# Four weight blocks taken in two passes behind the norms, and row block 5 of the attention outputs split around the memory heads

## The reference, cut to what matters

```python
for layer in range(DEPTH_2):
    # layer 0: NSA attention (compressed, selected, window), layer 1: MoBA attention
    q, ..., qm = split_cols(x @ w_in, sizes)
    o_mem = memory_attention(qm, mem, w_mem_kv)             # four heads on 256 memory rows
    mix = jnp.concatenate([o_main, o_mem], axis=-1) @ w_out # 1024 rows of w_out: 768 main, 256 memory
    x = layer_norm(ALPHA * x + mix, ln1_g[layer], ln1_b[layer])
    a, b = jnp.split(x @ ffn_w_in[layer], 2, axis=-1)
    ffn = (jax.nn.gelu(conv(a)) * b) @ ffn_w_out[layer]
    x = layer_norm(ALPHA * x + ffn, ln2_g[layer], ln2_b[layer])
```

## Time and profile before

| what | value |
|---|---|
| median of 3 runs | 958.37 us (957.88 to 958.4) |
| the profiled execution | 958.25 us |
| its span, first to last instruction | 956.6 us |
| TensorE matmul busy | 928.9 us, 97% |
| VectorE busy | 659.4 us, 69% |
| ScalarE busy | 527.2 us, 55% |
| mean granted TensorE clock | 0.994 |

### The profile page before, as it was taken

How to read it: one execution, slowest core, us unless ns; L and a number is a source line. 1 busy time by engine, 2 the same in 40 slices (tenths; PEclk the granted TensorE clock), 3 DMA queues, 4 the chain that set the end, 5 groups by cost and what they waited for, 6 DMA issues and landing times.

```text
span 956.6 us, 19717 instructions
## 1 busy us (share of the span) xinstructions
PE 928.9 (97%) x7025; PEld 844.7 (88%) x7025; DVE 659.4 (69%) x1258; ACT 527.2 (55%) x967; POOL 65.6 (7%) x119
## 2 busy tenths in 40 slices
PE   7999999999999999989999999999999999999995
PEld 4899999999999988667899999998988699999995
DVE  6466666666767777985886666668577796666665
ACT  5455555555544567764755455556665565555553
POOL 1000000000000001550100000001000100000001
PEclk9999999999999999999999999999999999999998
DMA  7555555556566666323566555565654447555641
GB/s 240 183 180 190 175 178 183 171 195 225 186 195 191 243 214 200 116 62 110 176 200 240 189 187 194 189 196 174 189 183 158 157 159 237 188 197 185 195 157 44
DMA packets 48233, 172.98 MB, mean 181 GB/s; under 512 B 6032, under 2 KB 6480, under 8 KB 48061
## 3 DMA queue, kind: packets, MB, share of 16 engines
q1 hardware_dynamic: 44732, 159.78, 50.7%
q0 software_dynamic: 3456, 12.61, 4.3%
HBM read 171.29 MB, written 1.07 MB: 180 GB/s over the span
## 4 chain that ended last, share of the span: by engine, by line
PE 86%; DVE 7%; ACT 3%; issue 2%; DMA 1%; POOL 0%; SPq 0%; POOLq 0%; DVEq 0%; ACTq 0%
PE bank L1411 18%; PE bank L1412 18%; PE bank L1410 18%; PE ysum L1481 6%; PE ysum L1483 6%; PE ysum L1482 6%; DVE sb_wl L830 2%; PE bank L1530 1%; PE ysum L1537 1%; PE ysum L1544 1%; PE ysum L1458 1%; PE ysum L1462 1%; PE ysum L1459 1%; DMA sb_raw<-in_stream 1%; ACT sb_xh L463 1%
## 5 line engine op out<-in xcount | busy, mean ns | idle before, releaser
L1411 PE MATMUL bank<-sb_xl,sb_wh 128*128 128x256 f32 x1360 | 377.9, 278 | 0.0
L1412 PE MATMUL bank<-sb_xh,sb_wl 128*128 128x256 f32 x1360 | 375.8, 276 | 0.0
L1410 PE MATMUL bank<-sb_xh,sb_wh 128*128 128x256 f32 x1332 | 370.5, 278 | 1.4 <-DVE sb_wl L830 1.4
L830 DVE TENSOR_TENSOR sb_wl<-sb_raw,sb_wh 128x1024 fp32r<-128x1024 f32 x201 | 245.3, 1223 | 111.9 <-ACT sb_wh L436 110.6
L436 ACT ACTIVATE sb_wh<-sb_raw 128x1024 fp32r<-128x1024 f32 x201 | 211.2, 1055 | 102.4 <-PE ysum L1483 43.4
L1410 PEld LDWEIGHTS bank<-sb_xh,sb_wh 128*128 128x128 f32 x1332 | 250.2, 188 | 6.4 <-issue 4.1
L1412 PEld LDWEIGHTS bank<-sb_xh,sb_wl 128*128 128x128 f32 x1360 | 255.5, 188 | 0.0
L1411 PEld LDWEIGHTS bank<-sb_xl,sb_wh 128*128 128x128 f32 x1360 | 255.5, 188 | 0.0
L830 DVE TENSOR_TENSOR sb_wl<-sb_gates,sb_wh 128x1024 fp32r<-128x1024 f32 x66 | 80.8, 1224 | 18.6 <-ACT sb_wh L436 18.6
L1482 PE MATMUL ysum<-sb_wl,sb_mh 128*128 128x512 f32 x208 | 81.1, 390 | 0.0
L1483 PE MATMUL ysum<-sb_wh,sb_ml 128*128 128x512 f32 x208 | 81.1, 390 | 0.0
(11 more groups left out here) (275 smaller groups left out, 1488.1 us busy)
## 6 DMA issues: line engine op xcount, KB each, us to landing
sb_raw<-in_stream SPq DMA_DIRECT2D x201, 512.0 KB, 3.4
sb_gates<-in_stream SPq DMA_DIRECT2D x66, 512.0 KB, 3.5
sb_t_dg<-in_stream SPq DMA_DIRECT2D x33, 512.0 KB, 4.1
sb_bias<-rel_rows POOLq DMA_DIRECT2D x12, 384.0 KB, 3.9
sb_bias<-in_alibi POOLq DMA_DIRECT2D x8, 256.0 KB, 3.1
sb_gb<-in_ln_g POOLq DMA_DIRECT2D x4, 512.0 KB, 5.0
sb_gb<-in_ln_b POOLq DMA_DIRECT2D x4, 512.0 KB, 6.5
sb_x_tok<-in_x SPq DMA_DIRECT2D x2, 512.0 KB, 3.7
```

The lines of the kernel that those rows point to most:

```text
L830: dve.tensor_tensor(wl[slot_of(b)][:, :, :], raw[home_of(b)][:, :, :], wh[slot_of(b)][:, :, :].bitcast(F32), ALU.subtract).then_inc(split_ ...
L1410: pe.matmul(out, wh[slot][:, k, :], mov_h(k), start=k == 0, stop=False)
L1411: pe.matmul(out, wh[slot][:, k, :], mov_l(k), start=False, stop=False)
L1412: last = pe.matmul(out, wl[slot][:, k, :], mov_h(k), start=False, stop=k == KT - 1)
```

## The change

Only TensorE's list is changed. Four blocks are taken in two passes: first all products with the high half of the weight, after a wait for `split_h` alone, then those with the low half, after `ready`. These are NSA block 2 behind n1 (it was the first of the two `wide` blocks), FFN block 2 behind n2 and behind n4, and MoBA value block 1 behind n3. In `finish`, row block 5 is split: tile 0, then the memory heads' output, then tile 1; `used` is counted after tile 1. The number and shapes of the matmuls stay.

```diff
+            def stationary_in_two(b, out, mov_h, mov_l):
+                sl = slot_of(b)
+                pe.wait_ge(split_h, b + 1)
+                for k in range(KT):
+                    pe.matmul(out, wh[sl][:, k, :], mov_h(k), start=k == 0, stop=False)
+                    pe.matmul(out, wh[sl][:, k, :], mov_l(k), start=False, stop=False)
+                ready(b + 1)
+                for k in range(KT):
+                    last = pe.matmul(out, wl[sl][:, k, :], mov_h(k), start=False, stop=k == KT - 1)
+                last.then_inc(used, 1)
+            def wide_in_two(b, part, bk, sh, sl):
+                ...            # the same for a wide block: 16 with wh, ready(b + 1), 8 with wl
+            def x_rows_in_two(nm, b, parts, out):
+                ...
+                for k, j, t, n in parts:
+                    x_ready(nm)(k)
+                    tok = slice(t * P, (t + 1) * P)
+                    pe.matmul(out(t, n)[:, :], xh[:, k, tok], part(wh, j), start=False, stop=False)
+                    pe.matmul(out(t, n)[:, :], xl[:, k, tok], part(wh, j), start=False, stop=False)
+                ready(b + 1)
+                for k, j, t, n in parts:
+                    last = pe.matmul(out(t, n)[:, :], xh[:, k, t * P:(t + 1) * P], part(wl, j), start=False, stop=False)
+                last.then_inc(used, 1)
...
             two_stationary(b, "n1")
             pe.wait_ge(kv_free, 2)
-            for n in range(2):
-                ready(b + n + 3)
-                wide(slot_of(b + n + 2), n, bank[2], xh, xl)
+            wide_in_two(b + 2, 0, bank[2], xh, xl)
+            ready(b + 4)
+            wide(slot_of(b + 3), 1, bank[2], xh, xl)
...
                 memory_turn(ph, 1)
-                rows(5)
+                ready(r0 + 6)
+                row_tile(slot_of(r0 + 5), oh[:, 5, :], ol[:, 5, :], 0, False, False)
                 memory_out(ph, 1)
+                row_tile(slot_of(r0 + 5), oh[:, 5, :], ol[:, 5, :], 1, False, False).then_inc(used, 1)
                 last_rows(r0 + 6, (oh[:, 6, :], ol[:, 6, :]), (oh[:, 7, :], ol[:, 7, :]), half, (), ((S[ph, "ol"], 2),))
...
             def ffn(ph, b0, nm):
                 two_stationary(b0, nm)
                 pe.wait_ge(kv_free, 4)
-                for n in range(2, 4):
-                    ready(b0 + n + 1)
-                    stationary(slot_of(b0 + n), bank[n][:, 0:T], xm, xml)
+                stationary_in_two(b0 + 2, bank[2][:, 0:T], xm, xml)
+                ready(b0 + 4)
+                stationary(slot_of(b0 + 3), bank[3][:, 0:T], xm, xml)
...
             for n in range(4):
                 b = B_MOBA + n
-                ready(b + 1)
-                x_rows("n3", slot_of(b), [(2 * n + j, j, t, 0) for j in range(2) for t in range(NT)],
-                       lambda t, n: bank[5 + t])
+                parts = [(2 * n + j, j, t, 0) for j in range(2) for t in range(NT)]
+                if n == 1:
+                    pe.wait_ge(split_h, b + 1)
+                    x_rows_in_two("n3", b, parts, lambda t, n: bank[5 + t])
+                else:
+                    ready(b + 1)
+                    x_rows("n3", slot_of(b), parts, lambda t, n: bank[5 + t])
```

More of the change, by code:

```diff
@@ L1414, in stationary @@
                     last.then_inc(used, 1)
+            def stationary_in_two(b, out, mov_h, mov_l):
[9 more added lines that the diff above has]
+            def wide_in_two(b, part, bk, sh, sl):
+                s = slot_of(b)
+                at = [(t, j) for t in range(NT) for j in range(KT // 2)]
+                pe.wait_ge(split_h, b + 1)
+                for t, j in at:
+                    k = part * KT // 2 + j
+                    hw = wh[s][:, 2 * j:2 * j + 2, :].rearrange("p k c -> p (k c)")
+                    for x in (sh, sl):
+                        pe.matmul(bk[:, t * T:(t + 1) * T], x[:, k, t * P:(t + 1) * P], hw,
+                                  start=k == 0 and t == 0 and x is sh, stop=False)
+                ready(b + 1)
+                for t, j in at:
+                    k = part * KT // 2 + j
+                    lw = wl[s][:, 2 * j:2 * j + 2, :].rearrange("p k c -> p (k c)")
+                    last = pe.matmul(bk[:, t * T:(t + 1) * T], sh[:, k, t * P:(t + 1) * P], lw,
+                                     start=False, stop=k == KT - 1 and t == NT - 1)
+                last.then_inc(used, 1)
             def two_stationary(b, nm):
@@ L1463, in x_rows, with part @@
                                      start=False, stop=k == KT - 1)
+                last.then_inc(used, 1)
+            def x_rows_in_two(nm, b, parts, out):
+                def part(w, j):
+                    return w[slot_of(b)][:, 4 * j:4 * j + 4, :].rearrange("p k c -> p (k c)")
+                for k, j, t, n in parts:
[6 more added lines that the diff above has]
+                    last = pe.matmul(out(t, n)[:, :], xh[:, k, t * P:(t + 1) * P], part(wl, j), start=False, stop=False)
                 last.then_inc(used, 1)
```

## The result

| | before | after |
|---|---|---|
| median | 958.01 us (6 runs, 955.75 to 958.4) | 962.25 us (6 runs, 961.25 to 965.06) |
| ratio | 1 | 1.0042, 95% interval 1.0025 to 1.0058 |
| span of the profiled execution | 956.6 us | 960.7 us |
| mean granted TensorE clock | 0.994 | 0.994 |

Slower by 0.42%, or 4.0 us (2.4 to 5.6). 961.2 was predicted, slower by more than 0.2% with a chance of 0.80. The direction and the place were right; the size was short: the span grew by 4.1, where 2.9 were forecast, and the median lies just above the top of the stated range, 962.2.

What follows compares the result with a forecast made beforehand. TensorE, busy 97% of the span at nearly full clock, was taken as the bound, so only its waits could move. 2 × 1.60 − 0.30 + 0 + 0 = +2.90 on 958.37 gave 961.27, stated as 961.2; range 959.8 to 962.2.

Steps and rivals of the forecast that it cites:

- Row block 5, the mechanism: Attention outputs: later last matmul delays the buffer release, ScalarE and row block 7; early output unused; 1.60 us each time.
- The bare cost of putting the output ahead: Row block 5: memory output ahead of its second half costs 1.12, plus 0.11 for a longer first matmul, 1.23 us.
- the copy's wait: Memory output inside row block 5: second head waits for VectorE's copy of its probabilities, 0.37 us of new waiting.
- its second head at +0.46: Memory output inside row block 5: second head placed 0.46 us after the output's start at 450.63, at 451.09.
- Behind n1 and n3: NSA block 2 and MoBA block 1: waits belong to the next, unsplit block, so the gain is 0.
- the pin: FFN loop's first column waits for its own low half, which doesn't move, so little of the 0.84 us stays.
- the −0.15: FFN block 2 behind n2 and n4: gain kept at each place, bounds 0 and 0.84 us.
- the sum of −0.30: Both FFN splits, behind n2 and n4, together: −0.30 us, between 0 and −1.68.
- Rival 1: FFN blocks behind n2 and n4: the gain stays whole, 1.68 us, giving 959.9; chance 0.09.
- Rival 2: Attention outputs: ScalarE takes the memory output before waiting for row block 5, so not slower, 957.9; chance 0.05.
- Rival 3: TensorE's clock falls after the new waits before row block 7, giving +6.3 us, 964.6; chance 0.06.
- Rival 4: Whole kernel: the change does nothing, splits off the path and row block 5 absorbed, 958.4; chance 0.03.

Runs made afterwards that it cites:

- e5: Kernel before with row block 5 split as in the change, and VectorE's copy of the second head's probabilities moved ahead of its weight's low half; ratio 1.0039.
- e7: Kernel before with one memory head's output between the halves of row block 5, the other behind it; 960.39 us, single run.
- e8: Kernel before with two passes for NSA block 3 behind n1 and MoBA block 2 behind n3 only; ratio 0.9987.
- e4: Kernel before, row block 5 whole, with ScalarE and VectorE taking the memory output's parts ahead of the next weight's halves; ratio 0.9990.
- e6: Kernel before with row block 5 split, second head's copy made early, and memory output's parts taken ahead of the next weight's halves; ratio 0.9988.
- e10: Kernel before with the change's FFN edit, and VectorE's four leftover norm steps one loop iteration later; ratio 0.9992.
- e1: The change without its row block 5 edit, only the four two-pass blocks behind the norms; 957.15 us, ratio 0.9989 against the kernel before.
- e9: Kernel before with swapped output and weight lists, two passes at NSA block 3 and MoBA block 2, and the change's FFN edit; 955.69 us, ratio 0.9978.
- e11: e9 plus VectorE's four leftover norm steps one iteration later in the FFN loops; 955.54 us, ratio 0.9966 against the kernel before.
- e3: Kernel before with row block 5 split, copy still late, and memory output's parts taken ahead of the next weight's halves; ratio 1.0009.
- e2: Kernel before with only the change's split of row block 5, norms as before; 962.88 us, ratio 1.0047.

## Why the prediction was right, and where its size was off

**Row block 5, the mechanism: right.** Everything from its last matmul on kept its distances (0.42 and 3.22 for 0.44 and 3.23), no engine used the early output, and nothing gave the loss back. The bare cost of putting the output ahead, forecast at 1.12 + 0.11 = 1.23, is what e5 and e7 show: 1.25 and 1.23.

**Row block 5, the mis-sized term: the copy's wait.** I put 0.37 and bounded the whole by 1.70; the wait cost 0.86 in pm3 (2.09 − 1.23) and 0.89 in pm5 (2.12 − 1.23), and the whole 2.1. The output began when I said (450.63 + 0.22 = 450.85), and the copy ended when I said (451.61). What failed is "its second head at +0.46": I took the second head for the second half of 1.02 us. It isn't; it lies beside the first and takes 1.01 by itself. Once it is held back, 1.88 us pass from the output's start to the next matmul, for my 1.39. What misled was a plausible spacing: eight matmuls of 256 columns in 1.02 us is 0.13 each, close to the 0.113 of the sixteen in the earlier trace rows, and looked like one behind the other. No row printed above contradicts it, but the trace of before does: its eight records start in pairs, and the eight loads in 0.64 us, 0.08 each, are closer together than that. Of the 1.2 us between the forecast and the span this is twice about 0.5; 0.2 were there before pm3 began.

**Behind n1 and n3: right, 0.** Both waits stayed (1.06 and 1.13 for 1.03 and 1.13), since they belong to the next block; e8 shows what they were worth, 0.28 and 1.40.

**Behind n2 and n4: the pin right, the −0.15 not shown.** The column is pinned by its low half, as forecast, and at least half of the 0.84 did not stay. But 0.13 less against one profiled execution of before, for my 0.15, can't be put down to the split. In e4, e5, e6, e7 and e8, whose FFNs are untouched, the column too stands 10.92 to 10.94 us after the sixteen low-x matmuls (before 11.16, after 10.93), with the same longer first matmul. The pace of TensorE differs from one execution to the next: the 48 matmuls of FFN blocks 2 and 3 take 5.73 us in before, and 5.53 and 5.52 in e8 and e7, the same code. Over the whole first FFN, by the same two events as for e10, the eight executions with an untouched FFN take 188.09 to 188.50, and the three with the split alone (after, e1, e9) 188.11 to 188.13; over the second, 178.16 to 178.61 and 178.13 to 178.25. So what the split itself is worth, from nothing to some 0.4 each, stays open, and that the sum of −0.30 looks close to the −0.26 seen is luck as far as the runs tell. e10 and e11 lie below all of these (187.73 and 187.76; 177.87 and 177.86): with VectorE's list relieved ahead of the column it does come earlier.

**The rivals.** Rival 1 (the gain whole) fell with the pin. Rival 2 can be seen in e3 and e6: with the lists swapped the wait before row block 7 goes, as it described, but the change doesn't do that. Rival 3, the clock: the granted clock over 452 to 460 and over 758 to 762 was 1.00, the higher level of 2.4 GHz, so the two new waits of 1.46 cost their length alone. The page of the Trainium skill that the prediction names there, "TensorE: Matmul & The Clock Gate", section "Why this matters for your kernels", warns of longer gaps than these. So the prediction's "by that rule alone" read too much into it. Rival 4 fell with the result.

## What to carry to other kernels

An output that is ready earlier gains nothing while its consumer stands behind another wait in its engine's list; moving the producer without moving the consumer only pushes back what the list does wait for, here by 1.25 us a time. Where two short groups of matmuls use different halves of the array's columns, as the two heads here, don't price one as half of the pair, and don't let a wait come between them. A split goes into the block whose own low half is late; after it, ask which next low half the freed engine runs into (behind n1 it took back 0.75 of 1.03, behind n3 nothing).

## What the runs showed of the hardware that was not expected

**Two heads of 64 columns side by side.** Eight matmuls take 1.02 us when the heads are adjacent, and four take 1.01 when a head is alone.

**A spell of the lower clock that some executions have and others not.** In the NSA part, which no kernel here touches, TensorE waits some 1.4 to 1.8 us for VectorE (the wait ends between 384.5 and 388.4). In 9 of the 13 profiled executions the mean granted clock from 387 to 392 is below 1.00 (0.66 to 0.77), in the other 4 (before, after, e5, e8) it is 1.00. The kernel before, and then e9 (start and end, length, busy times of PE, PEld, DVE, ACT and POOL, clock, DMA share, GB/s):

```profile
384.00:387.00 3.00, 1.55 (x14) 0.69 (x13) 2.90 (x12) 3.00 (x14) 0.34 (x1) 1.00 0.61 122
387.00:392.00 5.00, 5.00 (x47) 3.91 (x48) 4.86 (x29) 2.33 (x10) 4.15 (x6) 1.00 0.57 194
```

```profile
384.00:387.00 3.00, 1.37 (x16) 0.81 (x12) 2.86 (x13) 2.62 (x12) 0.00 (x0) 1.00 0.81 214
387.00:392.00 5.00, 5.00 (x34) 3.58 (x31) 4.26 (x21) 1.96 (x7) 4.76 (x8) 0.66 0.46 160
```

In e9 the clock was down to 0.66 on average, partly at 1.2 GHz, and 34 matmuls were done where 47 were before; from this wait to the next took 10.13 us, before 8.64: 1.5 us. TensorE was busy for about half of the 3 us from 384 to 387, which hold the wait, in both (1.55, 1.37). Why one execution falls and another doesn't stays open. It is as large as the effects studied here, so the spans of single executions don't rank such kernels; distances inside them do it better, though those across a whole FFN differ by 0.4 as well. The waits at row block 7, six of 1.46 or 1.47 us in three kernels (after, e2, e5), never showed it.
